# Selection counted in four pieces a bit, one index-score product, and the block sums of the output stage moved from GpSimd to VectorE

## What is computed

```python
for l in range(2):
    p = split_proj(rmsnorm(x, g_norm[l]) @ w_in[l])      # 1024 -> all q, k, v, gates
    # A: indexer scores, top-k keys per query, attention over these keys
    score = einsum('bqh,bqhl->bql', wi * H_IDX ** -0.5, relu(einsum(qi, ki) * 64 ** -0.5))
    top_s, top_i = lax.top_k(where(admissible, score, -inf), topk)   # 256 of up to 1024; sample 132 of 528
    # B: forgetting attention; C: chunk band attention; M: cross attention into 256 memory rows
    parts = [o_a, o_b, o_c, o_m] * silu(gate columns of p)
    x = x + concatenate(parts) @ w_out[l]                # (rows x 1024) @ (1024 x 1024)
y = rmsnorm(x, g_final)
```

## Time and profile before

| what | value |
|---|---|
| median of 3 runs | 1695.43 us (1693.01 to 1697.52) |
| profiled execution, its own time | 1695.91 us |
| its span, first to last instruction | 1694.1 us |
| mean granted TensorE clock | 0.997 |
| PE busy | 1657.6 us, 98% |
| PEld busy | 1116.2 us, 66% |
| DVE busy | 1083.6 us, 64% |
| ACT busy | 626.7 us, 37% |
| POOL busy | 321.7 us, 19% |

### The profile page before, as it was taken

How to read it: one execution, slowest core, us unless ns; L and a number is a source line. 1 busy time by engine, 2 the same in 40 slices (tenths; PEclk the granted TensorE clock), 3 DMA queues, 4 the chain that set the end, 5 groups by cost and what they waited for, 6 DMA issues and landing times.

```text
span 1694.1 us, 28367 instructions
## 1 busy us (share of the span) xinstructions
PE 1657.6 (98%) x9815; PEld 1116.2 (66%) x9815; DVE 1083.6 (64%) x2829; ACT 626.7 (37%) x1509; POOL 321.7 (19%) x500
## 2 busy tenths in 40 slices
PE   9999999999999999999999999999999999999998
PEld 4466666766677755588754666666666777556885
DVE  5747888788877334455445288887888773354454
ACT  3532334333343444422134323343333434445221
POOL 2242321100001022223021423220000010223110
PEclk9999999999999999999999999999999999999999
DMA  9343324123222341112251523241233132412021
GB/s 341 150 172 97 128 94 144 42 78 107 91 86 97 112 120 37 69 38 88 99 175 51 166 83 129 91 144 41 78 110 103 71 122 97 117 31 82 1 100 62
DMA packets 46382, 171.32 MB, mean 101 GB/s; under 512 B 11473, under 2 KB 11953, under 8 KB 43041
## 3 DMA queue, kind: packets, MB, share of 16 engines
q1 hardware_dynamic: 29632, 130.68, 22.8%
q0 software_dynamic: 16608, 38.83, 7.0%
HBM read 141.83 MB, written 30.73 MB: 102 GB/s over the span
## 4 chain that ended last, share of the span: by engine, by line
PE 63%; DVE 27%; issue 4%; ACT 3%; ACTq 1%; DVEq 1%; DMA 1%
PE psX L1113 32%; DVE lower L1572 15%; PE psX L1142 11%; PE psT L1026 6%; PE psX L1317 5%; PE psS L1250 4%; DVE work L1834 4%; PE psS L1169 2%; ACTq L1463 1%; DVE gate L1652 1%; PE psX L1026 1%; DVE work L1832 1%; ACT work L1504 1%; ACT gate L1377 1%; DVE gate L1848 1%
## 5 line engine op out<-in xcount | busy, mean ns | idle before, releaser
L1113 PE MATMUL psX<-wring,hT 128*128 128x512 f32 (+2 forms) x1504 | 609.5, 548 | 4.2 <-ACT qT L1423 2.6
L1113 PEld LDWEIGHTS psX<-wring,hT 128*128 128x128 f32 x1504 | 272.4, 191 | 222.4 <-issue 214.3
L1572 DVE TENSOR_SCALAR_CACHE_REDUCE lower<-sc,thr 128x640 uint8<-128x640 f32 (+5 forms) x462 | 407.3, 933 | 16.9 <-issue 9.0
L1113 PE MATMUL psX<-hT,wring 128*128 128x256 f32 (+1 forms) x1600 | 328.3, 359 | 4.5 <-ACT gate L1462 3.6
L1504 ACT ACTIVATE work<-work,stat 128x256 f32<-128x256 f32 (+7 forms) x288 | 200.0, 695 | 315.9 <-DVEq L1837 313.1
L1113 PEld LDWEIGHTS psX<-hT,wring 128*128 128x128 f32 x1600 | 274.2, 190 | 37.3 <-issue 8.2
L1513 ACT COPY work<-psT 128x512 f32<-128x512 f32 (+2 forms) x352 | 157.3, 488 | 295.2 <-PE psT L1026 292.8
L1026 PEld LDWEIGHTS psT<-con,work 128*128 128x128 f32 x1080 | 121.9, 141 | 77.0 <-issue 54.7
L1026 PE MATMUL psT<-con,work 128*128 128x128 f32 x1080 | 160.1, 279 | 10.9 <-DVE bias L1872 7.1
L1834 DVE CUSTOM_DVE_ANT_0 work<-psS,bias 128x640 f32<-128x640 f32 (+7 forms) x120 | 86.2, 718 | 39.1 <-issue 23.7
L1882 POOL DMA_DIRECT2D scratch_oscr<-gate x54 | 30.7, 569 | 346.2 <-DVEq L1868 294.3
(11 more groups left out here) (272 smaller groups left out, 1953.8 us busy)
## 6 DMA issues: line engine op xcount, KB each, us to landing
wring<-in_w SPq DMA_DIRECT2D x16, 2048.0 KB, 8.5
cache<-in_kB SPq DMA_DIRECT2D x16, 512.0 KB, 6.1
cache<-in_vB SPq DMA_DIRECT2D x16, 512.0 KB, 4.0
cache<-in_kC SPq DMA_DIRECT2D x16, 512.0 KB, 6.1
cache<-in_vC SPq DMA_DIRECT2D x16, 512.0 KB, 4.8
scratch_oscr<-gate POOLq DMA_DIRECT2D x54, 128.0 KB, 2.0
hT<-scratch_oscr SPq DMA_DIRECT2D x18, 384.0 KB, 3.0
kv<-in_x SPq DMA_DIRECT2D x9, 512.0 KB, 6.1
```

The lines of the kernel that those rows point to most:

```text
L1113: mm = pe.matmul(out, lhs, rhs, start=(kt == 0), stop=(kt == KT - 1))
L1572: v.tensor_scalar(lower[:, at:at + STRIP_L[t]], sc[:, o], thr[:, n:n + 1], 0.0, ALU.is_lt, ALU.add, accum_out=below[:, n:n + 1])
```

## The change

It has three parts.

1. The seven strips of a bit are counted in four steps (`bit`, `second`, `third`, `fourth`: strips 7 and 2; 6 and 3; 5 and the sample's; 4), each with its drain, where there were two (7, 6, 3; the sample's, 5, 4, 2). `project` calls `select` four times a unit with a quarter of `pace`.
2. One `iw` for all four pairs takes the place of two for two pairs each. The relus of pairs 2 and 3 go to places in `gate`. DVE copies 128 partitions once.
3. `Tw` and `Sh` are made by DVE. They wait in a list `sums`; `add_sums(2)` emits two ahead of the last `P` of a unit (and one more pair inside units with two packs), `add_sums(1)` one behind each `G`.

```diff
-FIRST, REST = [NT - 1, NT - 2, 3], [ST_, 5, 4, 2]
+COUNTED = [[7, 2], [6, 3], [5, ST_], [4]]
...
-    out = [(kind, i) for i in range(32) for kind in ("bit", "rest")]
+    out = [(kind, i) for i in range(32) for kind in ("bit", "second", "third", "fourth")]
...
+    sums = []
+
+    def add_sums(n):
+        for _ in range(n):
+            if sums:
+                emit(*sums.pop(0))
...
-        time = pace[0] / (4 if two_packs else 2)
+        time = pace[0] / 4
         select(time)
...
             odd_heads()
             select(time)
+            add_sums(2)
             emit("Pp", c, t, 3, 4)
...
             operands()
+            select(time)
             emit("Pp", c, t, 2, 5)
         odd_heads()
         select(time)
+        add_sums(2)
         emit("P", c, t)
+        if not two_packs:
+            select(time)
...
-        emit("iw", 0)
         emit("P", "B1", ST_)
...
-                emit("iw", 2)
+                emit("iw")
...
-                if c == "A2" and due and (l, (kind, at, 0)) not in o:
-                    for i in range(4):
-                        emit(kind, at, i)
+                if c == "A2" and due and (kind, at) not in begun:
+                    begun.append((kind, at))
+                    sums.extend((kind, at, i) for i in range(4))
...
                 emit("G", c, p, n)
+                add_sums(1)
...
-            if c == "O1" and p < 2:
-                for i in range(4):
-                    emit("Sh", p + 2, i)
+            if (c, p) in (("O1", 0), ("O0", 2)):
+                sums.extend(("Sh", 2 + p // 2, i) for i in range(4))
...
                     if (c, p) == ("O0", 0):
-                        for i in range(4):
-                            emit("Tw", "O1", i)
+                        sums.extend(("Tw", "O1", i) for i in range(4))
...
+            if s[0] == "is" and s[1] >= 2:
+                return gate[:, 4 * s[1] - 8:4 * s[1] - 4, :].rearrange("p a b -> p (a b)")
+            return buf(n_work[l, s] % 2)
...
                     for c0, c1 in ((0, PAST), (PAST, SKEYS)):
-                        for j in both:
+                        for j in range(PAIRS):
                             mm = pe.matmul(S.ap(s)[32 * j:32 * j + 32, c0:c1], wsel[:, j, :],
-                                           buf(n_work[l, ("is", j)] % 2)[:, c0:c1], start=True, stop=True)
+                                           index_buf(l, ("is", j))[:, c0:c1], start=True, stop=True)
...
+                elif k == "Tw":
+
+                    c, i = s[1:]
+                    if i == 0:
+                        dve.wait_ge(*w_loaded[chunks.index((l, c)) % 2].on(c))
+                    v.tensor_tensor(*w_sum(c, i), ALU.subtract)
+                    dve.drain().then_inc(w_combined.sem, 1)
+                elif k == "Sh":
+
+                    p, i = s[1:]
+                    if i == 0:
+                        dve.wait_ge(*k_stored.on("mm"))
+                        dve.wait_ge(*v_stored.on(("mm", 1)))
+                        dve.wait_ge(*sm_stored.on("s"))
+                        for t in (2 * p, 2 * p + 1):
+                            dve.wait_ge(*o_loaded[t].on("o"))
+                    v.tensor_tensor(*row_sum(p, i))
+                    dve.drain().then_inc(rows_combined.sem, 1)
...
                     if i < 32:
-                        count_below(FIRST)
+                        count_below(COUNTED[0])
                         dve.drain()
-                elif k == "K" and s[1][0] == "rest":
-                    count_below(REST)
+                elif k == "K" and s[1][0] in ("second", "third", "fourth"):
+                    count_below(COUNTED[("second", "third", "fourth").index(s[1][0]) + 1])
                     dve.drain()
...
-                    g.tensor_tensor(out, a, b, ALU.subtract).then_inc(w_combined.sem, 1)
-                    pool.drain()
...
-                    g.tensor_tensor(*row_sum(p, i))
-                    pool.drain().then_inc(rows_combined.sem, 1)
```

More of the change, by code:

```diff
@@ L167, in program_order @@
     count = lambda part: sum(STRIP_L[t] / 960 + 0.25 for t in part)
-    cost = lambda x: {"bit": 0.5 + count(FIRST) * (x[1] < 32), "rest": count(REST)}.get(
-        x[0], {"equals": 1.9, "ranks": 2.2, "mask": 2.4}.get(x[0], 0) * STRIP_L.get(x[1], 0) / 960 + 0.5)
+    cost = lambda x: {"bit": 0.5 + count(COUNTED[0]) * (x[1] < 32), "second": count(COUNTED[1]), "third": count(COUNTED[2]),
+                      "fourth": count(COUNTED[3])}.get(x[0], {"equals": 1.9, "ranks": 2.2, "mask": 2.4}.get(x[0], 0) * STRIP_L.get(x[1], 0) / 960 + 0.5)
     def select(time):
@@ L357, in program_order @@
         units += [("M1", t) for t in [ST_] + TILES[:NT]] + [("A2", t) for t in A2_ORDER]
+        begun = []
         for c, t in units:
@@ L832, in row_sum, with w_sum @@
                     (s4, upper[:, LAST_LINES, :], s2, ALU.subtract)][i]
+        def w_sum(c, i):
+            t1, t2, t3, t4 = w_sums[c]
+            b11, b12 = [w_quarter(c, FIRST_LINES, h) for h in range(2)]
+            b21, b22 = [w_quarter(c, LAST_LINES, h) for h in range(2)]
+            return [(t1, b12, b11), (t3, b22, b12), (t2, b22, t1), (t4, b21, t2)][i]
         def w_quarter(c, rows_, half):
@@ L1193, in _ @@
                 elif k == "iw":
-                    both = [s[1], s[1] + 1]
-                    for j in both:
+                    for j in range(PAIRS):
                         pe.wait_ge(*relued.on(("is", j)))
@@ L1486, in _ @@
                     act.wait_ge(*S.fill(s).on(s))
-                    if n >= 2:
+                    if k == "is" and s[1] >= 2:
+                        act.wait_ge(*normed.on(10))
+                    elif n >= 2:
                         pl, pv = [x for x in n_work if n_work[x] == n - 2][0]
@@ L1492, in _ @@
                         else:
-                            use = ("iw", pv[1] // 2 * 2)
-                            act.wait_ge(*S.fill(use, pl).on(use, pl))
-                    nc.scalar.activation(buf(n % 2)[:, 0:L], S.ap(s)[:, 0:L], ACT.Relu).then_inc(S.empty(s).sem, 1)
+                            act.wait_ge(*S.fill(("iw",), pl).on(("iw",), pl))
+                    nc.scalar.activation(index_buf(l, s)[:, 0:L], S.ap(s)[:, 0:L], ACT.Relu).then_inc(S.empty(s).sem, 1)
                     act.drain().then_inc(relued.sem, 1)
@@ L1974, in out_rows @@
                     return rows(d["p" + name], l, SEQ, t * P, P)
[L1976 to L2010 removed]
+                if k == "G" and s[3] == 6:
                     c, p, _ = s[1:]
```

41 lines of the change are left out of this document (5 added, 36 removed).

## The result

The changed kernel takes 1727.83 us (median of 4 runs, 1724.0 to 1728.52), the kernel before 1695.97 on the same chips: a ratio of 1.0184 (95% interval 1.0172 to 1.0196), 32 us slower. The forecast was no change, 1695.5 in a range of 1684 to 1707. The profiled execution of the changed kernel took 1728.48 us, with a span of 1726.7 and a mean granted clock of 0.993 (0.997 before).

The account below looks back on a forecast made before the run. PE, busy for 1657.6 of 1694.1 us, was taken as the bound, so terms counted as PE work or PE waits. Gains of −7.0, −5.1, −1.0, −2.4 and costs of +3.5, +1.0, +1.5, +9.5 summed to 0: 1695.5 us, range 1684 to 1707.

Parts of the forecast that it names:

- Waits that go: End of A2 units: without POOL's sums, PE's wait for the sample's gate multiplication goes, −3.5 us a layer, −7.0.
- clock: Behind those two long waits: TensorE's granted clock no longer falls, 3.4 and 1.7 us regained, −5.1.
- A2 pairs: Pairs of weight sums on DVE ahead of the gate steps of A2 units: some 0.75 us shows a layer, +1.5.
- Rival C: End of A2 units: the long waits stay, 7.0 + 5.1 us are not won, 1708; chance 0.05.
- Norm: L1615, stretched beside two of POOL's row sums, and PE's wait for the addition behind it: −1.0 us.
- Index sums: On PE, one merged index product costs about what one of two did, 1.2 us saved a layer, −2.4.
- Weight sums of O1: Four sums on DVE behind the first additions of (O0, 1) delay PE's `G` 6 by 1.75 us a layer, +3.5.
- Row sums of pair 2: On DVE, these sums now stand between norms and additions in (O1, 1): +1.0 us over both layers.
- Boundaries: Selection on DVE: 64 more piece boundaries a layer at 0.17 us make PE late by 4.75 a layer, +9.5; upper bound 21.8.
- rival A: Selection: boundaries don't reach PE, four calls a unit leave no long piece to wait behind; 1686.4, chance 0.24.
- Rival B: Selection: waits at 176 and 254 and their twins grow to 2 or 3 us, four clock falls add 10.2; 1706, chance 0.22.

Follow-up runs that it names:

- tw0_pool: `spread` with the four weight sums of O0 given back to POOL at their old place; 1699.58 us, ratio 1.0021 to the kernel before.
- spread: `two_two` with the weight sums of O1 put on the list ahead of (O0, 0) instead of behind it; 1689.16 us, ratio 0.9953 to the kernel before.
- two_two: The changed kernel with the old selection: two pieces a bit and two calls a unit; 1692.57 us, ratio 0.9981 to the kernel before.
- iw_two: `two_two` with the two index-score products of before instead of the single one; 1692.48 us, ratio 0.9968 to the kernel before.
- hd_ahead: `half_drains` with the quarter of selection behind the last projection step `P` moved ahead of it; 1687.12 us, ratio 0.9944 to the kernel before.
- half_drains: The changed kernel with unread flags written alternately to two places, so 128 drains go; 1706.03 us, ratio 1.0060 to the kernel before.
- part 4: Moved the selection quarter behind `P` in `half_drains`: ahead of `P` 1687.12 us, to the next unit's start 1708.74; compared PE's waits for ACT's copies.
- four_two: The changed kernel with four pieces a bit but the selection called at the two old places of a unit; 1704.12 us, ratio 1.0050 to the kernel before.
- hd_two_calls: `half_drains` with the selection called at the two old places of a unit; 1687.18 us, ratio 0.9941 to the kernel before.

## Why the prediction was wrong

- **Waits that go (−7.0) and clock (−5.1): right.** The waits are gone and the clock is whole in both layers; `tw0_pool`, with only these four sums back on POOL, takes 10.4 us more, where 12.1 less the 1.5 of the A2 pairs were forecast. Rival C falls with it. (One reading was off without harm: L1552 is a multiplication.)
- **Norm (−1.0): right**, the lag falls by 1.07 us at PE's matmul of 1632 us.
- **Index sums (−2.4): wrong, 0.** The product's own cost was right, 1.2 us merged or not. What was missed is the wait behind it: the next projection needs weights whose transfer is started by PE's own progress and lands some 10 to 12 us later. I named no work that becomes the bound when PE comes there sooner.
- **Weight sums of O1 (+3.5): right.** 1.71 us at the place where 1.75 were forecast; 4.7 us by the ratios of `spread` and `two_two`.
- **A2 pairs (+1.5): right**, 0.84 us in each layer, at the matmul of 702 us.
- **Row sums of pair 2 (+1.0): at most 0.7.** The lag grows from 12.6 us at 760 to 12.9 at 829 in layer 0, and from 33.2 at 1586 to 33.6 at 1625 in layer 1.
- **All of these together** were forecast at −9.5. `two_two`, which has them without the new selection, is 3.2 us (1.7 to 4.9) faster than the kernel before; `iw_two`, without the index term, 5.4 (3.6 to 7.1) where −7.1 was forecast. Without the index term most of the forecast is there; what the rest is, no run tells.
- **Boundaries (+9.5): the step that failed, in two ways.** First, the 128 drains cost 21 to 22 us, all of the upper bound. I had followed the lateness through the B units, correct to 0.1 us at pack (B, 1) (1.99 us where 2.06 were forecast), and then let it fade in the C units "whose tiles leave DVE more idle time". They don't take it up: of the lag of layer 0, 3.6 us had come by the end of the B units, about what I had worked out, and 13 came behind them, where I had put 0.7. The idle time there lies ahead of steps that wait for ACT or PE; at the gate step it is 56.7 us with the 128 drains and 56.6 without them, so they did not fill it. That a late DVE makes PE late and the idle time moves along is my reading of this. With two calls a unit the same 128 drains cost 1704.1 − 1687.2 = 16.9, by the ratios 18.5. Second, the places of the calls had no term at all. I read the two additional `select` calls as finer pacing that at worst costs the strip that stands ahead of pack (B, 1), and in rival A even as a gain. They cost 1706.0 − 1687.2 = 18.9 (20 by the ratios), because in DVE's fixed order a quarter of the unit's selection was put behind the gate step whose wait it had been filling: `hd_ahead`, which differs from `half_drains` in that quarter alone, has all of it back. The view that shows it was there: the group of L1652 has an idle time of its own, 33.8 us behind ACT, and it is selection work that keeps it from being more. With the 5.4 us that the finer pieces win, 21.8 + 18.9 − 5.4 = 35.3 are the 35.2 between `two_two` and the change. That is so by the way the differences are taken and proves nothing; in another order the shares are others, since the calls cost 27.5 with two pieces and the drains 16.9 with two calls.
- **Rival B (1706) was half right.** The clock did fall in the selection, at four places of 1.7 us, 6.8 in all; but the largest part of the loss is waiting, not a slower clock. The waits ahead of these falls were 1.85 to 2.59 us, between the 1.3 and 3.5 that I had to go by.
- **Rival A (1686.4)** needed free boundaries. The Trainium skill (VectorE: DVE Perf Modes, section "The DRAIN you can't avoid") says that a semaphore behind each of eight copies costs no more than one behind the last. No run here adds a semaphore alone; what the change adds at a boundary is an explicit drain, another thing, for which the prediction took that rule in this rival, and it does cost: the same passes took 21.8 us less with 128 of them removed. What the rival said of finer pieces has something in it, the 5.4 us above.
- **Open:** why finer pieces gain, and how the loss in the change itself divides. Its list of PE's waits has both kinds of part 4 (8.1 us for the copies of the projection, 18.9 for those of the transposed rows) and 7.9 us for the gate multiplication of the sample, which `half_drains` has at 0.2. Between `four_two` and `hd_two_calls`, which differ in the drains, it is 5.4 us more for the copies of the projection and 6.7 more for the gate multiplication, of 16.9 in all.

## What to carry to other kernels

In a program with a fixed order, filler work has its value from what it stands ahead of: put it in front of a step that waits long for another engine, not ahead of one that others wait for, and count how much stands in each stretch between such steps before and after the change. In this kernel a quarter of a unit's selection moved out of the right stretch cost some 20 us, to whichever side it went. Where the engine with the filler is near saturation and another engine waits for it, expect an added fixed cost to be paid nearly in full (17 to 22 of 21.8 us here), and look for what a step that becomes earlier will wait for next. A move from one engine to another is best judged by undoing it for one group alone: of the sums, four instructions a layer were worth 10 us, and the four of O1 cost 4.7 where they stood.

## What the runs showed of the hardware

- A drain of DVE between two counting passes costs 0.17 us; without it the next pass starts with the read-out of the one before. Over 128 of them that was 17 to 22 us of kernel time (`half_drains` against the change, `hd_two_calls` against `four_two`).
- The granted clock does not follow the length of the wait alone. Behind a wait of 2.43 us that began at 255.5 it fell, and 1.7 us were lost (the row of 256 to 264, 0.79). Behind one of 2.54 us at 175.9 and one of 2.64 at 1117.6 it stayed at 1.00:

```profile
178.00:184.00 6.00, 5.61 (x16) 2.77 (x17) 4.56 (x14) 2.35 (x5) 4.32 (x8) 1.00 0.73 229
1120.00:1126.00 6.00, 5.75 (x31) 5.09 (x32) 4.83 (x14) 1.95 (x5) 0.55 (x1) 1.00 0.07 25
```

- Beside subtractions of 128x1024 on POOL, two of VectorE's instructions with two operands in SBUF (L1575, a multiplication, and L1580, a subtraction, both 128x32) took 1.98 and 2.17 us in `tw0_pool`, 1.97 and 2.17 in the kernel before, and 0.19 in the changed kernel, which has no such subtraction on POOL.
